# Six folds of the decode samples' projection, moved from VectorE adds to TensorE matmuls

## The chip, the cores and the metric

The kernel runs on one core of one Trainium2 chip. The metric is the device time of one execution in microseconds, and lower is better. A run's figure is the median of several executions.

## What is computed

The program is one inference step of a hybrid decoder layer. It has 1024 prompt rows and 8 decode samples (one token each). Every row of both kinds goes through the same combined input projection, and its columns then feed two head groups:

```python
shift, scale, gate = ada_modulation(c, w_ada, b_ada)
h = x * (1.0 + scale) + shift
z = h @ w_in                      # 1024 -> 2480 columns
cq, ckv, kr, g_mla, gq, gk, gv, glr, g_gla = jnp.split(z, offs, axis=-1)
q = rms_norm(cq, q_norm_g) @ w_uq          # latent attention, 8 heads
ckv, kr = rms_norm(ckv, kv_norm_g), apply_rope(kr, cos, sin)
mla = attention(q, ckv, kr) * silu(g_mla)
gla = rms_norm(gated_linear_attention(gq, gk, gv, log_sigmoid(glr @ w_gate_up + b_gate))) * silu(g_gla)
out = layer_norm(alpha * x + gate * (concat(mla, gla) @ w_out))
```

The change touches only the projection `h @ w_in` of the 8 samples. Everything is float32; the prompt's projection is made of three products of split operands (high times high, high times low, low times high).

## The kernel before

The order of the work on each engine is written out by hand, and semaphores (`wait_ge`, `then_inc`) tie the engines together. Each engine works through its own list strictly in order.

The input projection has six chunks of columns (`NCH`), of 416, 512, 512, 512, 272 and 256 columns (`WIDTH`). In chunk c, TensorE makes eight row tiles t of 128 prompt rows (`rows_projected(c, t)`, L1885, 24 matmuls each) into PSUM banks 0 to 5. ScalarE copies each tile out (`copy_tile`, L980). Between tiles the same engine also gets small pieces of other work:

- `samples_part(c + 1)` (L1858) projects the 8 samples on the raw weights of the next chunk. It makes eight matmuls with a 32-column stationary operand. The eight pieces of the inner dimension are spread over four groups of 32 partitions in PSUM bank 6, so that the samples' result is the sum of four partial results, on partitions 0 to 7, 32 to 39, 64 to 71 and 96 to 103.
- VectorE makes that sum: a copy (L1369) and three adds (L1372), each on 8 partitions, into `zs`. `sproj_part` counts the four steps, and `samples_part` of the chunk after waits for it, since it writes bank 6 again.
- `split_w` on ScalarE (L915) and `low_w` on VectorE (L1311) make the high and the low part of the next chunk's weights. VectorE's `low_w` stands behind the samples' sum in its list.
- `gate_samples` on ScalarE (L948) applies SiLU to `zs` in chunks 1 and 3.

In chunk 1 VectorE also normalizes the latent columns (L1379 to L1401), after `latent_norms` on ScalarE (L957 to L975).

Two other places of the kernel before already use the constant `fold`, a matrix of 128 by 32 with a one at each partition 32g + b, column b, so that `fold` transposed times a tile adds up its four groups of partitions: L2230 and L2478 make one and two such matmuls of 512 columns. A float32 matmul is recorded as two matmul records.

Of the kernel before, what the change touches and what calls it, by code (L numbers as in the profile page):

```python
# [104 lines left out]
def hybrid_step(nc, a, o):  # L105

    with ExitStack() as ctx:
# [67 lines left out]
        def carve(n, *dims, rows=P, at=None, region=None):  # L175

            region = C if region is None else region
            start = taken[0] if at is None else at
            taken[0] = start + n
            v = region[0:rows, start:start + n]  # L180
            if len(dims) > 1:
                names = "abcd"[:len(dims)]
                v = v.rearrange(f"p ({' '.join(names)}) -> p {' '.join(names)}",
                                **{k: d for k, d in zip(names, dims)})
            return v
# [10 lines left out]
        carve(512, region=F)  # L196
# [235 lines left out]
        sproj_gated = sem("sproj_gated")  # L432
# [471 lines left out]
        def _(act):  # L904
# [40 lines left out]
            def gate_samples(c):  # L945
                act.wait_ge(sproj_part, 4 * c + 4)
                cols = zs[:, CHUNKS[c][0]:CHUNKS[c][1]]
                nc.scalar.activation(cols, cols, ACT.Silu).then_inc(sproj_gated, 1)  # L948

            def latent_norms():  # L950
# [9 lines left out]
                act.wait_ge(sproj_part, 4)  # L960
# [22 lines left out]
            def copy_chunk(c):  # L983
                for t in range(T):
                    copy_tile(c, t)
                    if t == (3 if c == 0 else 2):
                        split_w(c + 1)
                    if c in (1, 3) and t == 0:
                        gate_samples(c)
# [292 lines left out]
            act.wait_ge(sproj_done, NCH + 1)  # L1282
# [16 lines left out]
        def _(dve):  # L1299
# [65 lines left out]
            for c in range(NCH):  # L1365
                n = WIDTH[c]
                cols = zs[:, CHUNKS[c][0]:CHUNKS[c][1]]
                dve.wait_ge(sproj_done, c + 1)
                nc.vector.tensor_copy(cols, banks[0:NB, 6, 0:n]).then_inc(sproj_part, 1)  # L1369
                for g in range(1, 4):  # L1370
                    dve.wait_ge(sproj_part, 4 * c + g)
                    nc.vector.tensor_tensor(cols, cols, banks[32 * g:32 * g + NB, 6, 0:n], ALU.add).then_inc(sproj_part, 1)  # L1372
# [370 lines left out]
            dve.wait_ge(sproj_done, NCH + 1)  # L1743
# [34 lines left out]
            dve.wait_ge(sproj_done, NCH + 2)  # L1778
# [24 lines left out]
        def _(pe):  # L1803
# [44 lines left out]
            def samples_part(c):  # L1848

                if c == 0:  # L1850
                    pe.wait_ge(hs_ready, 1)
                    brought(pe, 1, 4)
                else:
                    pe.wait_ge(w_in_in[c], 16)
                    pe.wait_ge(sproj_part, 4 * c)
                for kk in range(2):
                    for g in range(4):
                        last = nc.tensor.matmul(banks[32 * g:32 * g + 32, 6, 0:WIDTH[c]], hsT[:, 4 * kk + g, :],  # L1858
                                                w_raw[c][:, 4 * kk + g, :], start=(kk == 0), stop=(kk == 1))
                last.then_inc(sproj_done, 1)  # L1860

# [204 lines left out]
            for c in range(NCH):  # L2066
                for t in range(T):
# [8 lines left out]
                    if c == 0 and t == 3:  # L2076
                        samples_part(0)
                    if c + 1 < NCH and t == (5 if c == 0 else 2):
                        samples_part(c + 1)
                    if c == NCH - 1:  # L2080
                        if t == 0:
                            pe.wait_ge(proj_copied, T * (NCH - 1))
                            pe.wait_ge(sproj_part, 4 * NCH)
                            pe.wait_ge(sproj_gated, 2)
                            pe.wait_ge(const_in, N_CONST)
                            gate_rows(0)
# [436 lines left out]
```

## Time and profile before

| | before |
|---|---|
| median of 3 runs | 766.61 us (761.47 to 768.01) |
| profiled execution, its own time | 761.47 us |
| span of the profiled execution | 759.6 us |
| TensorE busy | 710.7 us, 94% of the span |
| VectorE busy | 354.3 us, 47% |
| ScalarE busy | 326.3 us, 43% |
| mean granted TensorE clock | 0.993 of full speed |

The span runs from the first to the last instruction; the execution's own time is 1.9 us longer. A matmul's recorded end is modelled, and matmuls overlap, so its price in a stream is read from the starts of its neighbours, not from its duration.

### The profile page before, as it was taken

What the parts mean: (1) busy time and instruction counts of PE and PEld (TensorE: products, weight loads), DVE (VectorE), ACT (ScalarE), POOL (GpSimd) and SP (SyncE); (2) the same over time, 40 slices, a digit from 0 to 9 for tenths busy, and PEclk for the clock granted to TensorE, in tenths of its full rate; (3) what the DMA queues carried; (4) which work ended last, traced back from release to release, by engine and by line L of the source; (5) the groups of instructions that cost most, each with busy time, mean ns of one, the idle gap of its engine ahead of it and who ended that gap; (6) DMA issues with size and microseconds to landing.
All of it is one profiled execution on the core that took longest, in us unless ns stands there. A gap on an engine that the chain in (4) does not pass through costs nothing.

```text
span 759.6 us, 16796 instructions
## 1 busy us (share of the span) xinstructions
PE 710.7 (94%) x7057; PEld 549.7 (72%) x7057; DVE 354.3 (47%) x774; ACT 326.3 (43%) x779; POOL 76.0 (10%) x113
## 2 busy tenths in 40 slices
PE   1699999999999999999989899999999999999995
PEld 1287878878789986777755577777668889668884
DVE  0372352030202025868666766675661111377967
ACT  2081471021203136776645555565666666602100
POOL 0000000000000010110121122002112443000000
PEclk9899999999999999999999999999999999999999
DMA  9992210302001011000010200021225996102332
GB/s 319 415 364 80 81 62 1 110 1 76 18 1 56 1 32 59 10 15 9 9 11 1 57 1 2 1 56 56 86 70 179 337 389 233 60 28 85 124 126 84
DMA packets 32086, 70.33 MB, mean 93 GB/s; under 512 B 6482, under 2 KB 17835, under 8 KB 29324
## 3 DMA queue, kind: packets, MB, share of 16 engines
q1 hardware_dynamic: 27386, 47.73, 18.8%
q0 software_dynamic: 4016, 20.97, 7.4%
q8 instruction: 57, 0.93, 0.5%
q10 hardware_dynamic: 610, 0.55, 0.3%
q14 instruction: 17, 0.14, 0.1%
HBM read 62.26 MB, written 6.07 MB: 90 GB/s over the span
## 4 chain that ended last, share of the span: by engine, by line
PE 85%; DMA 5%; DVE 4%; ACT 2%; SPq 2%; issue 1%; POOL 1%; DVEq 0%; ACTq 0%; POOLq 0%
PE banks L1885 28%; PE banks L2059 8%; PE banks L2164 4%; PE banks L2245 4%; DMA s_x<-in_x_prompt 3%; PE banks L2266 3%; PE banks L2028 3%; PE banks L2395 2%; PE banks L2397 2%; PE banks L2396 2%; PE banks L1965 2%; DMA s_temps<-in_cache_k_rope,s_idx 2%; PE banks L2378 2%; PE banks L2335 2%; PE banks L2354 1%; PE banks L2379 1%
## 5 line engine op out<-in xcount | busy, mean ns | idle before, releaser
L980 ACT ACTIVATE s_z<-banks 128x512 f32<-128x512 f32 (+3 forms) x48 | 24.5, 514 | 156.4 <-PE banks L1885 156.4
L1885 PE MATMUL banks<-s_w_parts,s_h_a 128*128 128x512 f32 (+3 forms) x352 | 81.0, 329 | 0.9 <-DVE s_h_a L1340 0.9
L1885 PE MATMUL banks<-s_w_parts,s_h_b 128*128 128x512 f32 (+3 forms) x352 | 80.1, 328 | 0.0
L1885 PE MATMUL banks<-s_z_r,s_h_a 128*128 128x512 f32 (+1 forms) x224 | 72.6, 389 | 0.0
L1885 PE MATMUL banks<-s_z_r,s_h_b 128*128 128x512 f32 (+1 forms) x224 | 71.8, 388 | 0.0
L1184 ACT ACTIVATE s_z<-banks 128x512 f32<-128x512 f32 (+1 forms) x88 | 41.3, 517 | 52.3 <-PE banks L2245 52.1
L1369 DVE COPY s_zs<-banks 8x512 f32<-8x512 f32 (+3 forms) x6 | 3.5, 576 | 123.7 <-PE banks L1858 123.7
L1885 PEld LDWEIGHTS banks<-s_w_parts,s_h_a 128*128 128x128 f32 x352 | 54.0, 189 | 8.1 <-issue 3.1
L1885 PEld LDWEIGHTS banks<-s_w_parts,s_h_b 128*128 128x128 f32 x352 | 54.0, 189 | 6.1 <-issue 1.5
L1885 PEld LDWEIGHTS banks<-s_z_r,s_h_a 128*128 128x128 f32 x224 | 42.0, 188 | 10.3 <-issue 1.7
L1175 ACT ACTIVATE s_z<-banks,s_temps 128x128 f32<-128x128 f32 (+7 forms) x64 | 47.1, 740 | 4.4 <-DVE s_temps L1636 3.7
L1885 PEld LDWEIGHTS banks<-s_z_r,s_h_b 128*128 128x128 f32 x224 | 42.0, 188 | 8.4
L2245 PEld LDWEIGHTS banks<-s_ident,s_z 128*128 128x128 f32 x288 | 33.5, 141 | 10.6 <-issue 5.4
L2245 PE MATMUL banks<-s_ident,s_z 128*128 128x128 f32 x288 | 39.7, 274 | 0.8 <-DVE s_z L1647 0.8
L2059 PE MATMUL banks<-s_kt,s_temps 96*128 96x512 f32 (+1 forms) x96 | 39.6, 534 | 0.0
L2164 PE MATMUL banks<-s_z 128*64 128x128 f32 x576 | 38.5, 278 | 0.8 <-ACT s_z L1184 0.8
L1194 ACT ACTIVATE s_z<-banks 128x512 f32<-128x512 f32 x64 | 33.1, 602 | 13.7 <-PE banks L2266 13.7
L2164 PEld LDWEIGHTS banks<-s_z 128*64 128x64 f32 x576 | 30.8, 136 | 6.2 <-issue 5.2
L1647 DVE TENSOR_SCALAR s_z<-s_z,s_temps 128x128 f32<-128x128 f32 (+7 forms) x64 | 33.3, 542 | 1.7
L1631 DVE TENSOR_REDUCE s_temps<-banks 128x1 f32<-128x640 f32 (+3 forms) x32 | 32.8, 1025 | 1.1
L2059 PE MATMUL banks<-s_kt,s_z 96*128 96x128 f32 (+2 forms) x96 | 32.3, 458 | 0.0
L1287 ACT ACTIVATE s_temps<-s_temps,s_eps_t 128x1 f32<-128x1 f32 (+1 forms) x9 | 2.7, 295 | 67.8 <-DVE s_temps L1766 67.8
(370 smaller groups left out, 1354.7 us busy)
## 6 DMA issues: line engine op xcount, KB each, us to landing
s_z<-in_w_ada SPq DMA_DIRECT2D x8, 1024.0 KB, 19.3
s_temps<-in_w_in SPq DMA_DIRECT2D x3, 2048.0 KB, 7.7
s_x<-in_x_prompt SPq DMA_DIRECT2D x8, 512.0 KB, 21.5
s_z<-in_w_ada SPq DMA_DIRECT2D x1, 4096.0 KB, 16.8
s_kt<-in_w_out SPq DMA_DIRECT2D x8, 512.0 KB
s_temps<-in_x_prompt SPq DMA_DIRECT2D x8, 512.0 KB
out_y_prompt<-s_temps SPq DMA_DIRECT2D x7, 512.0 KB
s_temps<-in_w_in SPq DMA_DIRECT2D x1, 1664.0 KB, 9.0
```

What stands on the lines that cost most here:

```text
L980: nc.scalar.activation(z[:, t, CHUNKS[c][0]:CHUNKS[c][1]], banks[:, proj_bank(c, t), 0:WIDTH[c]], ACT.Silu if c in (1, 3) else ACT.Copy).t ...
L1175: last = nc.scalar.activation(weights_of(s, u), score_of(s, u), ACT.Exp, bias=nmx[:, c:c + 1], accum_out=rsum[:, c:c + 1])
L1184: nc.scalar.activation(PTb[r % 3][:, 4 * g:4 * g + n, :], banks[:, 4 + (groups(r) + g) % 2, 0:P * n].rearrange("p (j q) -> p j q", j=n), A ...
L1194: nc.scalar.activation(latT(n, j), banks[:, j, :], ACT.Copy).then_inc(f_Tc, 1)
L1631: nc.vector.tensor_reduce(nmx[:, c:c + 1], score_of(s, 0), AX_X, ALU.max, negate=True).then_inc(mx_ready, 1)
L1647: last = nc.vector.tensor_scalar(weights_of(s, u), weights_of(s, u), rinv[:, c + u:c + u + 1], None, ALU.mult)
L1885: last = nc.tensor.matmul(banks[:, proj_bank(c, t), 0:WIDTH[c]], h_[half][:, k, n0:n0 + P], w_[c][:, k, :], start=(k == 0 and n == 0), sto ...
L2028: last = nc.tensor.matmul(banks[:, q_bank(i, q), 0:384], z[:, i, P * k:P * k + P], w_uq[:, k, 384 * q:384 * q + 384], start=(k == 0), stop ...
L2059: last = nc.tensor.matmul(score_of(s, u)[:, n0:n1], QTb[i % 2][:, h, :], KTh[:, h, n0:n1], start=True, stop=True)
L2164: last = nc.tensor.matmul(banks[64 * par:64 * par + 64, 6, 0:P], V(j, 2 * hp + par), block, start=(j == 0), stop=(j == i))
L2245: last = nc.tensor.transpose(banks[:, 4 + k0 % 2, P * (b % 4):P * (b % 4) + P], Pm[r % 3][:, P * b:P * b + P], ident[:])
L2266: last = nc.tensor.transpose(banks[:, j, P * r:P * r + P], cached(n, 4 * j + r), ident[:])
```

## The change

The sum of the four partial results moves from VectorE to TensorE. VectorE now makes one copy of all 128 partitions of bank 6 into SBUF (`zs_part`). TensorE multiplies it by `fold` (`samples_fold`) into bank 7, two row tiles after the samples' part (one tile after it for chunk 0). ScalarE copies the 8 rows from bank 7 into `zs` (`copy_samples`), with SiLU for chunks 1 and 3 on the way, in place of the separate SiLU. `sproj_done` now counts two steps for each chunk, and `sproj_copied` takes the place of `sproj_gated` and of the counts of `sproj_part`.

```diff
-        carve(512, region=F)
+        zs_part = carve(512, region=F)
...
-            def gate_samples(c):
-                act.wait_ge(sproj_part, 4 * c + 4)
-                cols = zs[:, CHUNKS[c][0]:CHUNKS[c][1]]
-                nc.scalar.activation(cols, cols, ACT.Silu).then_inc(sproj_gated, 1)
+            def copy_samples(c):
+                act.wait_ge(sproj_done, 2 * c + 2)
+                nc.scalar.activation(zs[:, CHUNKS[c][0]:CHUNKS[c][1]], banks[0:NB, 7, 0:WIDTH[c]],
+                                     ACT.Silu if c in (1, 3) else ACT.Copy).then_inc(sproj_copied, 1)
...
-                act.wait_ge(sproj_part, 4)
+                act.wait_ge(sproj_copied, 1)
...
-                    if c in (1, 3) and t == 0:
-                        gate_samples(c)
+                    if c == 0 and t == 5:
+                        copy_samples(0)
+                    if c == 1 and t == 0:
+                        copy_samples(1)
+                    if c >= 1 and t == (7 if c == 2 else 5):
+                        copy_samples(c + 1)
...
-                cols = zs[:, CHUNKS[c][0]:CHUNKS[c][1]]
-                dve.wait_ge(sproj_done, c + 1)
-                nc.vector.tensor_copy(cols, banks[0:NB, 6, 0:n]).then_inc(sproj_part, 1)
-                for g in range(1, 4):
-                    dve.wait_ge(sproj_part, 4 * c + g)
-                    nc.vector.tensor_tensor(cols, cols, banks[32 * g:32 * g + NB, 6, 0:n], ALU.add).then_inc(sproj_part, 1)
+                dve.wait_ge(sproj_done, 2 * c + 1)
+                nc.vector.tensor_copy(zs_part[:, 0:n], banks[:, 6, 0:n]).then_inc(sproj_part, 1)
...
-                    pe.wait_ge(sproj_part, 4 * c)
+                    pe.wait_ge(sproj_part, c)
...
+            def samples_fold(c):
+                pe.wait_ge(sproj_part, c + 1)
+                if c == 0:
+                    pe.wait_ge(mod_ready, 3)
+                else:
+                    pe.wait_ge(sproj_copied, c)
+                n = WIDTH[c]
+                nc.tensor.matmul(banks[0:32, 7, 0:n], fold[:], zs_part[:, 0:n], start=True, stop=True).then_inc(sproj_done, 1)
...
+                    if c == 0 and t == 4:
+                        samples_fold(0)
...
+                    if c + 1 < NCH and t == (7 if c == 0 else 4):
+                        samples_fold(c + 1)
...
-                            pe.wait_ge(sproj_part, 4 * NCH)
-                            pe.wait_ge(sproj_gated, 2)
+                            pe.wait_ge(sproj_copied, NCH)
```

The later waits on `sproj_done` are only renumbered.

On TensorE, in chunk 1, at the border from row tile 4 to row tile 5 (`s_z_r` and `s_w_parts` hold the weights' parts, `s_h_b` the second half of the rows), the list before is:

```order
L1885 MATMUL banks<-s_w_parts,s_h_b 128x512
L1885 MATMUL banks<-s_z_r,s_h_b 128x512
L1885 MATMUL banks<-s_z_r,s_h_b 128x512 [waits proj_copied]
L1885 MATMUL banks<-s_w_parts,s_h_b 128x512
L1885 MATMUL banks<-s_z_r,s_h_b 128x512 x2
```

and now it is:

```order
L1894 MATMUL banks<-s_w_parts,s_h_b 128x512
L1894 MATMUL banks<-s_z_r,s_h_b 128x512
L1869 MATMUL banks<-s_front,s_fold 32x512 [waits sproj_copied,sproj_part]
L1894 MATMUL banks<-s_z_r,s_h_b 128x512 [waits proj_copied]
L1894 MATMUL banks<-s_w_parts,s_h_b 128x512
L1894 MATMUL banks<-s_z_r,s_h_b 128x512 x2
```

One fold (L1869, reading `zs_part` in `s_front`) now stands between two tiles; nothing was taken from TensorE's list.

On VectorE, behind the normalization of chunk 1, the list before is:

```order
L1401 TENSOR_TENSOR s_zs<-s_zs,s_front 8x32 [waits kr_turned]
L1369 COPY s_zs<-banks 8x512 [waits sproj_done]
L1372 TENSOR_TENSOR s_zs<-s_zs,banks 8x512 [waits sproj_part] x3
L1311 TENSOR_TENSOR s_w_parts<-s_temps,s_z_r 128x2048 [waits w_hi_ready] x2
```

and now it is:

```order
L1401 TENSOR_TENSOR s_zs<-s_zs,s_front 8x32 [waits kr_turned]
L1372 COPY s_front<-banks 128x512 [waits sproj_done]
L1315 TENSOR_TENSOR s_w_parts<-s_temps,s_z_r 128x2048 [waits w_hi_ready] x2
```

The three adds are gone, and the copy goes to `s_front` on 128 partitions; it stands where the old copy stood, and the fold of chunk 2 waits for it.

## Rows read from the trace of the kernel before

**Rows 1.** Windows of the projection: us, busy us of each engine, clock, DMA
```profile
core 0: us, PE busy (x) PEld busy (x) DVE busy (x) ACT busy (x) POOL busy (x), PEclk, DMA share, GB/s
60.00:90.00 30.00, 30.00 (x184) 23.77 (x184) 10.84 (x12) 6.08 (x7) 0.00 (x0) 1.00 0.20 70
90.00:138.00 48.00, 48.00 (x218) 37.80 (x217) 14.92 (x32) 21.18 (x56) 0.00 (x0) 1.00 0.13 45
...
184.00:239.00 55.00, 55.00 (x295) 45.39 (x293) 4.13 (x6) 10.29 (x17) 0.00 (x0) 1.00 0.19 52
```

**Rows 2.** Waits from 60 to 257 us: us in total, times, longest
```profile
ACT s_z L980 <- PE banks L1885: 138.5, 34, 7.8
DVE s_zs L1369 <- PE banks L1858: 123.7, 5, 38.4
```

**Rows 3.** The chain that ended last, 60 to 275 us: shares and a piece
```profile
by line: PE banks L1885 92.8%; PE banks L1858 4.3%; PE banks L1844 1.7%; PE banks L1927 0.6%; PE banks L1942 0.2%; PE banks L1941 0.2%; PE banks L1922 0.2%; PE banks L1914 0.1%
...
109.29 44.57 PE banks L1885 x192
```

**Rows 4.** TensorE at chunk 1's start and a samples' part: start us, us, what
```profile
90.64 0.40 PE L1885 MATMUL banks<-s_z_r,s_h_a 128*128 128x512 f32 x1
...
106.81 0.39 PE L1885 MATMUL banks<-s_w_parts,s_h_a 128*128 128x512 f32 x1
107.04 0.40 PE L1885 MATMUL banks<-s_z_r,s_h_a 128*128 128x512 f32 x1
107.37 1.92 PE L1858 MATMUL banks<-s_temps,s_hsT 128*32 128x512 f32 x16
109.22 0.50 PE L1885 MATMUL banks<-s_z_r,s_h_a 128*128 128x512 f32 x1
109.56 0.39 PE L1885 MATMUL banks<-s_w_parts,s_h_a 128*128 128x512 f32 x1
```

**Rows 5.** Timeline of TensorE around the two folds of L2478
```profile
675.37 0.39 PE L2379 MATMUL banks<-s_z_r,s_w_parts 128*128 128x512 f32 x1
675.69 1.90 PE L2478 MATMUL banks<-s_z,s_fold 128*32 128x512 f32 x4
677.52 0.50 PE L2378 MATMUL banks<-s_z_r,s_w_parts 128*128 128x512 f32 x1
```

**Rows 6.** Timeline of TensorE around the single fold of L2230, and its durations
```profile
542.75 1.04 PE L2230 MATMUL banks<-s_z,s_fold 128*32 128x512 f32 x2
543.72 1.55 PE L2059 MATMUL banks<-s_kt,s_temps 96*128 96x512 f32 x3
...
L2230 PE MATMUL banks<-s_z,s_fold x2: 592/604/617, 542.7 to 543.2; 128*32 128x512 f32 x2
```

**Rows 7.** Timeline of TensorE in chunk 5, tiles 0 to 2
```profile
254.50 3.03 PE L1885 MATMUL banks<-s_w_parts,s_h_a 128*128 128x256 f32 x24
257.38 0.27 PE L1914 MATMUL banks<-s_ident,s_z 128*16 128x128 f32 x1
...
260.44 0.69 PE L1927 MATMUL banks<-s_w_gu,s_temps 17*128 17x256 f32 x2
...
264.04 0.27 PE L1914 MATMUL banks<-s_ident,s_z 128*16 128x128 f32 x1
```

**Rows 8.** VectorE: a group of the adds, and the timeline around the sums
```profile
L1372 DVE TENSOR_TENSOR s_zs<-s_zs,banks 8x512 f32<-8x512 f32 x9 | 6.1, 683 | 0.3
...
81.59 0.68 DVE L1369 COPY s_zs<-banks 8x512 f32<-8x512 f32 x1 [8.70 <-PE banks L1858]
...
84.35 4.47 DVE L1311 TENSOR_TENSOR s_w_parts<-s_temps,s_z_r 128x2048 fp32r<-128x2048 f32 x2
...
110.55 0.68 DVE L1369 COPY s_zs<-banks 8x512 f32<-8x512 f32 x1
```

**Rows 9.** ScalarE: timeline, and a copy of 8 rows out of PSUM
```profile
81.73 0.91 ACT L980 ACTIVATE s_z<-banks 128x416 f32<-128x416 f32 x2
...
L1278 ACT ACTIVATE s_zs<-banks x2: 569/570/572, 656.0 to 657.0; 8x512 f32<-8x512 f32 x2
```

More of the change, by code:

```diff
@@ L431, in hybrid_step @@
         sproj_done = sem("sproj_done")
-        sproj_gated = sem("sproj_gated")
+        sproj_copied = sem("sproj_copied")
         silu_done = sem("silu_done")
@@ L1281, in _ @@
             high_mixed(2)
-            act.wait_ge(sproj_done, NCH + 1)
+            act.wait_ge(sproj_done, 2 * NCH + 1)
             nc.scalar.activation(y_part, banks[:, 6:8, :].rearrange("p b n -> p (b n)"), ACT.Copy).then_inc(gate_bc, 1)
@@ L1742, in _ @@
             low_mixed(2)
-            dve.wait_ge(sproj_done, NCH + 1)
+            dve.wait_ge(sproj_done, 2 * NCH + 1)
             for k in range(KT):
@@ L1777, in _ @@
             r8, all_cols = slice(0, NB), slice(0, D)
-            dve.wait_ge(sproj_done, NCH + 2)
+            dve.wait_ge(sproj_done, 2 * NCH + 2)
             added(0, r8, all_cols, gateS, 6)
```

## The prediction

> **What bounds the kernel now.** I read the busy time by windows first, over the stretch from 60 to 239 us in which all six samples' sums are made or prepared. In each of the three windows shown TensorE's busy time equals the window (30 of 30, 48 of 48, 55 of 55 us), at full granted clock, 2.4 GHz [rows 1]. VectorE and ScalarE are busy for 4 to 15 us and 6 to 21 us there.
>
> Busy matmuls can still hide a wait, so the waits come second. From 60 to 257 us the list holds no TensorE matmul that waits for VectorE or ScalarE. It is the others that wait for TensorE: ScalarE 138.5 us for row tiles, and VectorE 123.7 us in total for the samples' parts, up to 38.4 us at a time [rows 2].  Third, the chain that ended last: from 60 to 275 us it lies on TensorE alone, 92.8% on the row tiles of L1885 and 4.3% on the samples' parts [rows 3]. A row tile of 512 columns takes 44.57 / 8 = 5.57 us in that chain.
>
> So the stage lasts as long as TensorE's list. Time taken from VectorE is worth nothing here unless TensorE would have waited for it, and time given to TensorE is paid in full.
>
> **What the change removes.** The 18 adds on VectorE go: nine of 512 columns take 6.1 us at 683 ns [rows 8], the other nine (416, 272 and 256 columns) about 3.8 us more, estimated by their columns. All of that lay in VectorE's slack, since VectorE then waited for the next samples' part. Worth of it on the path: 0. What could be late next is `low_w`, which stands behind the sum: for chunk 1 it ran from 84.35 for 4.47 us [rows 8], to 88.8, and chunk 1 starts at 90.64 [rows 4]. It was already in time by 1.8 us, and it now ends about 1 us earlier (3 x 0.68 = 2.0 us of adds less, 1.0 us of delay from the fold ahead of it). Two SiLU passes on ScalarE go too; they become part of the new copies. Worth 0.
>
> **What it adds on VectorE and ScalarE.** The copy grows from 8 to 128 partitions. Its bounds from the rows are 0.68 us for 512 columns on 8 partitions and about the same for an add of this length; partitions work side by side, so I take 0.68 us, hence no change. ScalarE gets six copies of 8 rows, less two SiLU passes; one of 512 columns out of PSUM took 570 ns [rows 9]. That is some 2 us net in an engine that waits 138.5 us for row tiles. Worth 0.
>
> **The new waits.** Each fold waits for VectorE's copy, and (from chunk 1 on) for ScalarE's copy of the chunk before. Behind it in TensorE's queue stand all row tiles, so a late partner would stop everything. The places, in the times of before:
> - Fold 1 stands after tile 7 of chunk 0, so just before 90.64 [rows 4] plus one us. VectorE's copy ends at about 82.3 [rows 8]. ScalarE's copy of chunk 0 stands behind the tile copies that began at 81.73 [rows 9] and ends near 83.2. Slack: 8 us.
> - Fold 2 is the tightest on VectorE, which holds it behind the latent normalization. The old copy started at 110.55 [rows 8], so the new one ends near 111.3, or near 112.5 with the delay of two folds. Its samples' part ended at 109.22 [rows 4] and two tiles of 5.57 us follow, so TensorE comes to the fold near 120.4, plus the same delay. Slack: 9 us.
> - For folds 3 to 5 VectorE is idle when the part ends, so the copy is done within 1 us of it, and two tiles follow, 11 us of 512 columns or 6 us of 272 columns (a 256-column tile lasts 257.38 - 254.50 = 2.88 us [rows 7]).
> - At the start of chunk 5 TensorE waits for all six sample copies. The last stands on ScalarE behind the copy of tile 5 of chunk 4 and ahead of two more tile copies for which TensorE already waits there. Nothing new.
>
> So all waits are met and cost 0. The transfers of the weights are issued after the same row tiles as before and slide with them.
>
> **What it adds on TensorE: six folds.** I price them by starts of neighbours. In the stream, a record of 512 columns starts every 0.23 us (106.81 to 107.04). Going into the samples' part that step is 0.33 us, and the second step after it is 0.34 us (109.22 to 109.56), so the two edges add 0.10 + 0.11 = 0.21 us [rows 4]. The two folds of L2478 hold the engine from 675.69 to 677.52, 1.83 us for four records [rows 5]; with the edges 2.04 us. The single fold of L2230 holds it from 542.75 to 543.72, 0.97 us for two records [rows 6]; with the edges 1.18 us. The difference of the two is two records: 0.86 us, 0.43 us each, and what is left over once for each insertion is 0.31 us.
>
> A fold of 512 columns is thus 0.86 + 0.31 = 1.17 us. By columns, 416 gives 0.70 + 0.31 = 1.01, 272 gives 0.46 + 0.31 = 0.77, and 256 gives 0.43 + 0.31 = 0.74. The last has a check: the small float32 matmul of 256 columns at L1927 stretched its tile from 2.88 us to 264.04 - 260.44 = 3.60 us, so 0.72 us [rows 7]. The sum:
>
> 3 x 1.17 + 1.01 + 0.77 + 0.74 = 6.0 us, all on the path.
>
> Bounds: without any cost at the edges it is 6.0 - 6 x 0.31 = 4.1 us. If the two records of a fold didn't overlap at all, each would take its recorded 0.60 us [rows 6] in place of 0.43; scaled by columns that adds 0.34 us for each 512 columns, over 2480 columns in all 1.6 us, so 7.7 us. I take 6.0, since the three places that it rests on agree within 0.03 us.
>
> The Trainium skill's "TensorEngine Tiling (Array Packing)", section Key Properties, says that changing the tiling mode drains the engine. The trace agrees: the 0.31 us are paid where 128*32 records stand between 128*128 ones. By the rule alone, folds placed right behind a samples' part, in the same mode, would save it and the sum would be near the lower bound; here each stands between two row tiles.
>
> **The sum.** The profiled execution took 761.47 us, so 767.5 us, a ratio of 1.0079. The median of the three runs shown is 766.61 us, and that execution was the fastest of the three. On the median the same 6.0 us give **772.6 us**, which I forecast. About 1% (7.7 us) is what a measurement of this kernel can tell from no change, so this is a loss that is just too small to be told with certainty.
>
> **Rivals.**
> 1. *The folds are hidden.* TensorE's weight loads are busy for 37.80 of 48 us, or 79% [rows 1], and in the samples' part 16 records of 512 columns take 1.85 us (107.37 to 109.22 [rows 4]), 0.12 us each, since four groups of 32 columns run side by side. If a fold's records cost only this, 12 of them cost 1.4 us and the time is 768.0 us, no change. Against it: all folds write the same group of 32 columns (partitions 0 to 31), they have no partner to run beside, and L2478 shows 0.43 us for such a record. The point from which it decides is whether the next row tile may start during a fold. The Trainium skill says in "Perfetto Trace Analysis", Identifying the Most-Contended Engine, that matmul busy time is a poor measure of how near TensorE is to its limit, and that weight-load busy time is a better one; by it there would be a fifth of room here, and this rival is what it would make of the change. The spacing of 0.23 us for 512 columns at full clock speaks against the room. Chance 0.06.
> 2. *The freed VectorE pays.* If the low weight parts had held TensorE at chunk borders, the adds would give up to 3 x 0.68 = 2.0 us back at each of five borders, 10.2 us against 6.0, so 762.4 us, faster. It decides if `low_w` ends after the chunk starts. It ends 1.8 us before at the border of chunk 1, the tightest, and no TensorE wait is listed. Chance 0.03.
> 3. *A fold stalls TensorE.* This ends clearly slower. The place is fold 2, where VectorE's copy is queued behind a normalization that itself waits for ScalarE. It decides once that copy ends later than 120 us, 9 us later than now; each us beyond is paid in full. With the copy 12 us later it would cost 3 us, in all 9 us and 775.6 us. Nothing in the change delays VectorE so much. Chance 0.03.
> 4. *The folds are dearer.* At the upper bound of 7.7 us the time is 774.3 us, at the border of 1%. This is the upper end of the forecast rather than another mechanism.
>
> **How the numbers follow.** The forecast, a pure cost on TensorE between 4.1 and 7.7 us, has 0.88. The runs shown differ by 6.5 us, so a median of a few can be off by 2 to 3 us either way; the centre of 6.0 lies 1.7 us below the 1% border, so about a quarter of the forecast's chance, 0.22, lies beyond it, and the rest, 0.66, within 1%. With rival 3 slower gets 0.25. Within 1% gets 0.66 + 0.06 = 0.72. Rival 2 with scatter makes 0.03 for faster. The range goes from the lower bound less 3 us of scatter (766.6 + 4.1 - 3 = 767.7), taken to 767 for rival 1, to the upper bound with 3.5 us of scatter (766.6 + 7.7 + 3.5 = 777.8): 767 to 778 us.
>
> **What would show it.** In the changed kernel's profile: six fold matmuls, two records each, with 0.97 us from the first one's start to the next row tile at 512 columns; no TensorE wait for VectorE or ScalarE from 60 to 257 us; the chunk starts later by 2.2 us at chunk 1 (folds 0 and 1), and chunk 5 by the whole 6.0 us; VectorE's busy time down by about 10 us with longer waits for the samples' parts; everything behind the projection unchanged in length and moved by 6 us. The prediction is wrong if a fold costs TensorE well under 1 us at 512 columns, if one of them waits, or if a later stage gives time back, which I can't see from here, since it starts only when TensorE has finished the projection.

## Result and profile after

| | before | after |
|---|---|---|
| median | 764.39 us (20 runs, 759.5 to 771.52) | 769.17 us (20 runs, 765.84 to 777.85) |
| ratio | | 1.0082, 95% interval 1.006 to 1.0103 |
| profiled execution, its own time | 761.47 us | 771.46 us |
| span | 759.6 us | 769.7 us |
| mean granted TensorE clock | 0.993 | 0.985 |

The change makes the kernel slower: by 0.8% by the ratio, whose interval reaches from 0.6 to 1.0%, and by 4.8 us or 0.6% by the two medians. The loss of about 6 us that was forecast is 0.8%, so it lies within that interval. It is within the 1% that a few runs can't tell from no change; with 20 runs of each it can be told. The two profiled executions differ by more, 10 us, and why is part of the study.

The windows of the projection after (columns as in [rows 1], bounds moved with the work):

```profile
60.00:90.00 30.00, 30.00 (x182) 23.19 (x175) 7.06 (x6) 6.34 (x8) 0.00 (x0) 1.00 0.20 70
91.00:144.00 53.00, 53.00 (x232) 40.22 (x232) 12.88 (x29) 21.60 (x57) 0.00 (x0) 1.00 0.17 59
184.00:244.00 60.00, 60.00 (x315) 48.66 (x314) 2.94 (x4) 11.23 (x18) 0.00 (x0) 1.00 0.16 48
```

The waits after, from 60 to 263 us:

```profile
ACT s_z L980 <- PE banks L1894: 145.8, 35, 7.8
DVE s_front L1372 <- PE banks L1858: 136.4, 5, 42.5
```

TensorE still fills each window at full clock (30 of 30, 53 of 53, 60 of 60 us), and the list still holds no matmul of it that waits for VectorE or ScalarE. It does hold six weight loads of row tiles (PEld, 4.2 us in all) that are put down to ScalarE's tile copies; they are the loads behind the six folds, and what they mean is told with e12. Against [rows 2] the other engines wait longer: ScalarE by 7.3 us, VectorE by 12.7 us, of which about 6 us are the longer stage. The time that the adds gave up has become waiting too.

The chain that ended last, after, from 60 to 281 us:

```profile
by line: PE banks L1894 90.7%; PE banks L1858 4.1%; PE banks L1869 2.2%; PE banks L1844 1.6%; PE banks L1936 0.6%; PE banks L1931 0.4%; PE banks L1951 0.2%; PE banks L1950 0.2%; PE banks L1923 0.1%
...
74.41 0.81 PE banks L1869 x2
...
91.09 0.98 PE banks L1869 x2
92.07 16.82 PE banks L1894 x72
...
122.03 0.97 PE banks L1869 x2
...
216.44 0.57 PE banks L1869 x2
```

In [rows 3] the row tiles and the samples' parts follow each other without a gap; now the folds of L1869 lie in the chain too, 2.2% of it.

TensorE's timeline after, around fold 1 and fold 2:

```profile
90.75 0.35 PE L1894 MATMUL banks<-s_w_parts,s_h_b 128*128 128x416 f32 x1
91.03 1.05 PE L1869 MATMUL banks<-s_front,s_fold 128*32 128x512 f32 x2
92.00 0.50 PE L1894 MATMUL banks<-s_z_r,s_h_a 128*128 128x512 f32 x1
92.34 0.39 PE L1894 MATMUL banks<-s_w_parts,s_h_a 128*128 128x512 f32 x1
...
121.63 0.40 PE L1894 MATMUL banks<-s_z_r,s_h_b 128*128 128x512 f32 x1
121.95 1.05 PE L1869 MATMUL banks<-s_front,s_fold 128*32 128x512 f32 x2
122.93 0.50 PE L1894 MATMUL banks<-s_z_r,s_h_b 128*128 128x512 f32 x1
123.27 0.40 PE L1894 MATMUL banks<-s_w_parts,s_h_b 128*128 128x512 f32 x1
```

The starts read as they did around L2230 and L2478 [rows 5, 6]. Fold 2 comes 0.32 us behind its neighbour (instead of 0.23), holds the engine for 0.98 us, and the step behind it is 0.34 us. Above the usual steps that is 0.09 + 0.98 + 0.11 = 1.18 us.

VectorE after, the group of the new copies (columns as in [rows 8]):

```profile
L1372 DVE COPY s_front<-banks 128x512 f32<-128x512 f32 (+3 forms) x6 | 3.5, 589 | 136.4 <-PE banks L1858 136.4
```

**The measure used below.** The whole time scatters by several us, so each experiment is read by a *stretch* of its chain first: from the start of the first gate-column matmul (L1844 in the kernel before) to the start of row tile 1 of chunk 5. It contains all six folds. Before it is 257.65 - 60.55 = 197.10 us, after it is 262.98 - 59.84 = **203.14 us**: 6.04 us more. Two further runs show how well it repeats: the kernel before once more gave 197.09 us, the changed one once more 203.13 us.

### The profile page after: what moved, and what is told of

Read it like the earlier page. It is cut to its first block, busy times and chain, and to the rows that moved or that the text cites. A ratio compares the mean times of both kernels' runs of the same rounds, so it can differ in the third digit from the quotient of the medians.

```text
span 769.7 us, 16811 instructions
## 1 busy us (share of the span) xinstructions
PE 723.2 (94%) x7069; PEld 553.8 (72%) x7069; DVE 343.9 (45%) x756; ACT 327.5 (43%) x783; POOL 75.5 (10%) x113
## 4 chain that ended last, share of the span: by engine, by line
PE 86%; DMA 4%; DVE 3%; ACT 2%; SPq 2%; issue 1%; POOL 0%; DVEq 0%; ACTq 0%; POOLq 0%
PE banks L1894 28%; PE banks L2068 8%; PE banks L2176 4%; PE banks L2257 4%; PE banks L2278 3%; DMA s_x<-in_x_prompt 3%; PE banks L2037 3%; PE banks L2407 2%; PE banks L2409 2%; PE banks L2408 2%; PE banks L1974 2%; PE banks L2347 2%; PE banks L2366 2%; PE banks L2390 2%; PE banks L2391 1%
## 5 line engine op out<-in xcount | busy, mean ns | idle before, releaser
L1372 DVE COPY s_front<-banks 128x512 f32<-128x512 f32 (+3 forms) x6 | 3.5, 589 | 136.4 <-PE banks L1858 136.4
L1894 PEld LDWEIGHTS banks<-s_z_r,s_h_b 128*128 128x128 f32 x224 | 42.0, 188 | 10.4 <-ACT s_z L980 1.7
```

Of the source, the lines that this page charges most:

```text
L1894: last = nc.tensor.matmul(banks[:, proj_bank(c, t), 0:WIDTH[c]], h_[half][:, k, n0:n0 + P], w_[c][:, k, :], start=(k == 0 and n == 0), sto ...
```

## Experiments

### The two halves of the change

**e1_folds_only**: the kernel before, with its adds, and six float32 folds of another tile into bank 7 at the places of the change. Their results are used by nobody.

```diff
+            def extra_fold(c):
+                if c == 0:
+                    pe.wait_ge(mod_ready, 3)
+                n = WIDTH[c]
+                nc.tensor.matmul(banks[0:32, 7, 0:n], fold[:], modB[:, 0:n], start=True, stop=True)
...
+                    if c == 0 and t == 4:
+                        extra_fold(0)
...
+                    if c + 1 < NCH and t == (7 if c == 0 else 4):
+                        extra_fold(c + 1)
```

> The kernel before with its VectorE adds kept, and six extra fold matmuls on a constant tile at the places of the changed kernel; their result is not used, and they wait for nothing but the gate's bias once. Measure: the stretch of TensorE from the first gate-column matmul (chunk 0) to row tile 1 of chunk 5, 197.1 us before and 203.1 us in the changed kernel. Theory A (the folds' TensorE time is the whole effect, 6.0 us; VectorE's and ScalarE's part is worth 0): 203.1 us, and 1.008 of the kernel before. Rival B (the folds cost more, say 8 us, and the freed VectorE or ScalarE gives 2 us back): 205 us, 1.0105. Rival C (the folds are free, and the loss comes from the new waits and copies): 197.1 to 198.5 us, 1.000 to 1.002.

Measured: stretch 203.14 us, the changed kernel's to 0.01 us. Median 774.04 us, ratio 1.012 (1.0071 to 1.0168).

**e2_no_adds**: the kernel before without its 18 adds. It leaves three of the four partial sums of the samples out; the waits on `sproj_part` are renumbered to fit.

```diff
                 nc.vector.tensor_copy(cols, banks[0:NB, 6, 0:n]).then_inc(sproj_part, 1)
-                for g in range(1, 4):
-                    dve.wait_ge(sproj_part, 4 * c + g)
-                    nc.vector.tensor_tensor(cols, cols, banks[32 * g:32 * g + NB, 6, 0:n], ALU.add).then_inc(sproj_part, 1)
```

> The kernel before without the 18 adds on VectorE: each samples' part is only copied from partitions 0 to 7, so three of the four partial sums are left out. Theory A: VectorE's time is off the path, the stretch stays 197.1 us, ratio 1.000. Rival B: the stretch is shorter by 1 to 2 us or a later stage gains, ratio 0.997 to 0.999. Either way VectorE's busy time falls by about 10 us.

Measured: stretch 197.09 us, median 764.69 us, ratio 0.999 (0.9968 to 1.0012). VectorE's busy time fell from 354.3 to 344.2 us and bought nothing. Its wait for the samples' parts (123.7 us in [rows 2]) took it up:

```profile
DVE s_zs L1369 <- PE banks L1855: 131.2, 5, 40.6
```

So the folds on TensorE are the whole cost, and the freed VectorE is worth nothing: rival 2 is out.

### What a fold's price consists of

**e3_folds_twice**: the changed kernel, each fold made twice in a row.

```diff
+                nc.tensor.matmul(banks[0:32, 7, 0:n], fold[:], zs_part[:, 0:n], start=True, stop=True)
                 nc.tensor.matmul(banks[0:32, 7, 0:n], fold[:], zs_part[:, 0:n], start=True, stop=True).then_inc(sproj_done, 1)
```

> The changed kernel with each fold made twice in a row (the second overwrites the first with the same values). Theory A (0.43 us for each record of 512 columns, and 0.31 us once for each place where a fold stands between row tiles): 12 more records but no new place, so 2480 columns x 2 x 0.84 ns = 4.2 us more than the changed kernel, stretch 207.3 us, 1.0135 of the kernel before. Rival D (the records cost little, the change of tile shape costs nearly all): 0.5 to 1.5 us more, 204 to 204.6 us. Rival E (each fold pays its own edge even when the next is also a fold): 6.0 us more, 209.1 us, 1.016.

Measured: stretch 207.27 us, 4.13 us above the change; ratio 1.0175 (1.0134 to 1.0216). Its timeline of TensorE at the start of chunk 1 (L1895 is the row tiles):

```profile
92.11 1.04 PE L1869 MATMUL banks<-s_front,s_fold 128*32 128x512 f32 x2
92.99 1.02 PE L1870 MATMUL banks<-s_front,s_fold 128*32 128x512 f32 x2
93.95 0.50 PE L1895 MATMUL banks<-s_z_r,s_h_a 128*128 128x512 f32 x1
```

An *edge* is what an insertion costs once, above its records, 0.31 us in the prediction. The second fold adds 0.88 us, and no edge. Twelve records more cost 4.13 us over 2480 columns, 0.43 us for a record of 512.

**e4_fold_beside_part**: folds 0 to 4 moved right ahead of the next samples' part, so that they share its edges; fold 5 stays. ScalarE's copies of the samples move with the folds (not shown).

```diff
-                    if c == 0 and t == 4:
-                        samples_fold(0)
                     if c + 1 < NCH and t == (5 if c == 0 else 2):
+                        samples_fold(c)
                         samples_part(c + 1)
-                    if c + 1 < NCH and t == (7 if c == 0 else 4):
-                        samples_fold(c + 1)
+                    if c == NCH - 2 and t == 4:
+                        samples_fold(NCH - 1)
```

> The changed kernel with folds 0 to 4 moved to stand right ahead of the next chunk's samples' part, so that 128*32 matmuls stand together; fold 5 stays alone. ScalarE's copies move with them. Theory A with the edge paid for changing the tile shape: five edges of 0.31 us saved, 1.5 us less than the changed kernel, stretch 201.6 us, 1.006 of the kernel before. Rival F (the 0.31 us belong to the float32 matmul itself or to its semaphore): nothing saved, 203.1 us, 1.008.

Measured: stretch 201.46 us, 1.68 us less than the change for five edges, 0.34 us each; ratio 1.0083 (1.0054 to 1.0111). Its timeline at the samples' part in chunk 1 (L1867 the fold, L1856 the part, L1892 the row tiles):

```profile
107.77 0.40 PE L1892 MATMUL banks<-s_z_r,s_h_a 128*128 128x512 f32 x1
108.09 0.62 PE L1867 MATMUL banks<-s_front,s_fold 128*32 128x512 f32 x1
108.11 0.63 PE L1856 MATMUL banks<-s_temps,s_hsT 128*32 128x512 f32 x3
108.55 0.59 PE L1867 MATMUL banks<-s_front,s_fold 128*32 128x512 f32 x1
108.56 2.29 PE L1856 MATMUL banks<-s_temps,s_hsT 128*32 128x512 f32 x13
110.79 0.50 PE L1892 MATMUL banks<-s_z_r,s_h_a 128*128 128x512 f32 x1
```

There is one step of 0.32 us in (107.77 to 108.09) and one of 0.33 us out (the next record of the row tile starts at 111.12) for both together.

**e7_gate_beside_part**: the kernel before, with the gate columns (L1844, float32, 128*32) moved down one tile, next to the first samples' part. No fold is in it: it asks whether an edge of the kernel before can be saved too.

```diff
-                    if c == 0 and t == 2:
-                        gate_columns()
                     if c == 0 and t == 3:
+                        gate_columns()
                         samples_part(0)
```

> The kernel before with the gate's columns moved from behind row tile 2 of chunk 0 to behind tile 3, right ahead of samples' part 0, so that two blocks of 128*32 matmuls stand together. Theory A (edges are paid where the tile shape changes): one edge less, 0.3 us less. Measured from the start of row tile 1 of chunk 0 to row tile 1 of chunk 5, 206.2 us before: 205.9 us. Rival (no such edge): 206.2 us. The whole execution can't tell either from no change.

Measured: since the gate columns move, the stretch is read from tile 1 of chunk 0, and it is 205.86 us against 206.19 before, 0.33 us less. Median 764.44 us, ratio 0.9991 (0.9965 to 1.0017). It is the only version that shortens the stretch of the kernel before by more than the 0.01 us to which it repeats; in the whole time so little can't be told.

**e6_fold_f32r**: the changed kernel with each float32 fold replaced by two fp32r products, of a high and a low part of `zs_part`, with an fp32r copy of `fold` as the stationary operand. VectorE makes the low part with one more operation.

```diff
-                nc.tensor.matmul(banks[0:32, 7, 0:n], fold[:], zs_part[:, 0:n], start=True, stop=True).then_inc(sproj_done, 1)
+                nc.tensor.matmul(banks[0:32, 7, 0:n], fold_r[:], zs_hi[:, 0:n], start=True, stop=False)
+                nc.tensor.matmul(banks[0:32, 7, 0:n], fold_r[:], zs_lo[:, 0:n], start=False, stop=True).then_inc(sproj_done, 1)
```

> The changed kernel with each float32 fold replaced by two matmuls of type fp32r, on the high and the low part of the copy; VectorE makes the low part with one more subtraction. Theory A (a record's price is its time in the array: 0.43 us for 512 float32 columns, 0.23 us for 512 fp32r columns as the row tiles show, and 0.31 us for the edges): 2480 columns x 2 x 0.45 ns = 2.2 us and 6 x 0.31 = 1.9 us, 4.1 us over the kernel before, stretch 201.2 us, 1.005 of the kernel before. Rival (each insertion has a fixed price whatever the type): 203.1 us, 1.008.

Measured: stretch 199.32 us, only 2.22 us above the kernel before, where 201.2 was expected; ratio 1.0058 (1.0028 to 1.0088). TensorE's timeline at the start of chunk 1 (L1874 and L1875 the products, L1900 the row tiles):

```profile
90.72 0.35 PE L1900 MATMUL banks<-s_w_parts,s_h_b 128*128 128x416 f32 x1
90.90 0.39 PE L1874 MATMUL banks<-s_front_parts,s_fold_r 128*32 128x512 f32 x1
91.13 0.39 PE L1875 MATMUL banks<-s_zs_lo,s_fold_r 128*32 128x512 f32 x1
91.36 0.40 PE L1900 MATMUL banks<-s_z_r,s_h_a 128*128 128x512 f32 x1
91.59 0.39 PE L1900 MATMUL banks<-s_w_parts,s_h_a 128*128 128x512 f32 x1
```

The steps run 0.18, 0.23, 0.23, 0.23 us. Each product costs what a record of a row tile costs, and there is no edge, though the records carry the same 128*32 as the folds. That was my miss: I had put the edge down to the form alone.

**e9_wide_float32**: the mirror case. The kernel before, with six float32 matmuls at the folds' places whose stationary operand has 128 columns (an identity). Their results are used by nobody.

```diff
+                nc.tensor.matmul(banks[:, 7, 0:n], ident[:], modB[:, 0:n], start=True, stop=True)
```

> The kernel before with six extra float32 matmuls at the folds' places and of the folds' column counts, but with a stationary operand of 128 columns (the identity), so that the tile shape 128*128 stays and only the type changes from fp32r to float32; the result is not used. The run with fp32r folds of shape 128*32 showed no edge at all, which speaks against the tile shape as its cause. Theory H (the 0.31 us at the edges are paid for a float32 matmul between fp32r ones): the stretch from the first gate-column matmul to row tile 1 of chunk 5 is 203.1 us, as with the folds. Theory A as first stated (paid for the change of shape): 197.1 + 4.2 = 201.3 us.

Measured: stretch 201.22 us, 4.12 us above the kernel before; ratio 1.0086 (1.0053 to 1.0119). The records cost what they cost in e3, and again there is no edge, so theory H is out. Neither float32 alone nor 32 columns alone brings the edge; among the added matmuls only the float32 ones of 32 columns have it.

**e12_padded_fold**: the same on the change's own folds: their stationary operand is padded with zeros to 128 columns.

```diff
+            nc.vector.tensor_copy(fold_w[:, 0:32], fold[:]).then_inc(mod_ready, 1)
+            nc.vector.memset(fold_w[:, 32:P], 0.0).then_inc(mod_ready, 1)
...
-                nc.tensor.matmul(banks[0:32, 7, 0:n], fold[:], zs_part[:, 0:n], start=True, stop=True).then_inc(sproj_done, 1)
+                nc.tensor.matmul(banks[:, 7, 0:n], fold_w[:], zs_part[:, 0:n], start=True, stop=True).then_inc(sproj_done, 1)
```

> The changed kernel with its folds' stationary operand padded from 32 to 128 columns (96 columns of zeros, made once on VectorE), so that the six folds keep their float32 records and places but are recorded as 128*128, like their neighbours. In the stretch of the chain from the first gate-column matmul to row tile 1 of chunk 5, the kernel before takes 197.1 us and the changed one 203.1. Theory A (0.43 us for a record of 512 columns, plus about 0.31 us once for each insertion of 32-column float32 records among 128-column ones): no insertion cost, so 197.1 + 4.1 = 201.2 us. Rival (the 0.31 us belongs to waiting on another engine's semaphore or to the place, not to the records' form): 203.1 us. In the whole time, about 768.5 against 764.4 for the kernel before, a ratio near 1.0055 by theory A and 1.008 by the rival, which the scatter may not tell apart; the stretch decides.

Measured: stretch 261.79 - 60.57 = 201.22 us, as theory A had it. Four times as many columns are computed and the fold is cheaper by 0.32 us. Since place, waits and data are those of the change, the edge belongs to the form of the records and not to a wait. Median 768.18 us, ratio 1.0098 (1.0065 to 1.013); that is more than the 1.0055 expected, and the part on the rest of the time comes back to it. Its timeline of TensorE at the start of chunk 1 (L1897 is the row tiles):

```profile
91.15 0.35 PE L1897 MATMUL banks<-s_w_parts,s_h_b 128*128 128x416 f32 x1
91.34 1.02 PE L1872 MATMUL banks<-s_front,s_fold_w 128*128 128x512 f32 x2
91.80 0.79 PE L1897 MATMUL banks<-s_z_r,s_h_a 128*128 128x512 f32 x1
92.43 0.39 PE L1897 MATMUL banks<-s_w_parts,s_h_a 128*128 128x512 f32 x1
```

From 91.34 to 92.43 there are 1.09 us for two records and one of a row tile, 0.86 + 0.23; the step in is the usual 0.19 us of a record of 416 columns, where the 32-column fold shows 0.28 us (90.75 to 91.03).

**What the weight loads show.** Each matmul record has a weight load ahead of it, listed under PEld. In the change, around fold 2:

```profile
121.41 0.19 PEld L1894 LDWEIGHTS banks<-s_z_r,s_h_b 128*128 128x128 f32 x1
121.95 0.14 PEld L1869 LDWEIGHTS banks<-s_front,s_fold 128*32 128x32 f32 x2 [0.36 <-issue]
122.93 0.19 PEld L1894 LDWEIGHTS banks<-s_z_r,s_h_b 128*128 128x128 f32 x1 [0.84 <-ACT s_z L980]
```

and in e12, around fold 1:

```profile
91.16 0.38 PEld L1872 LDWEIGHTS banks<-s_front,s_fold_w 128*128 128x128 f32 x2
91.77 0.19 PEld L1897 LDWEIGHTS banks<-s_z_r,s_h_a 128*128 128x128 f32 x1 [0.24 <-issue]
```

In a row tile a load starts a step ahead of its matmul (121.41 for 121.63). At the 32-column float32 fold it doesn't: the fold's load and matmul both start at 121.95, and the next row tile's both at 122.93, after the fold. With the padded fold the loads run ahead again (91.16 for 91.34, and 91.77 while the fold's second record is still under way), and so they do in e6 (90.72 and 90.91 for 90.90 and 91.13). So the edge comes with a load that isn't made during the matmul before it. The ScalarE named in the wait of 0.84 us is not its cause: the same gap stands behind the samples' part of the kernel before, with `issue` in its place (109.22).

The kernel before has another float32 record with this gap, L1927 of [rows 7], with 17 partitions and all 128 columns:

```profile
260.44 0.29 PEld L1927 LDWEIGHTS banks<-s_w_gu,s_temps 17*128 17x128 f32 x2
261.06 1.26 PEld L1885 LDWEIGHTS banks<-s_w_parts,s_h_a 128*128 128x128 f32 x10 [0.33 <-ACT s_z L980]
```

Both loads start with their matmuls (260.44 and 261.06), and the insertion costs the 0.72 us of the prediction, where e9's 128*128 insertion of 256 columns costs 0.43 us (249.23 to 249.67 in its chain). So among float32 records it isn't the 32 columns as such: 17 partitions bring an edge too.

### The cover of the waits

**e5_no_cover**: the changed kernel with each fold right behind its own samples' part, without the row tiles between them.

```diff
-                    if c == 0 and t == 4:
+                    if c == 0 and t == 3:
                         samples_fold(0)
...
                         samples_part(c + 1)
-                    if c + 1 < NCH and t == (7 if c == 0 else 4):
                         samples_fold(c + 1)
```

> The changed kernel with every fold made right behind its own samples' part, with no row tile between them. Theory A says that the two tiles between cover VectorE's copy: without them TensorE waits at each fold for the copy (0.58, three times 0.68, 0.43 and 0.41 us) and about 0.2 us of signalling, 4.7 us in all, and at fold 2 for VectorE's normalization too, about 1.3 us, while the folds lose one edge each (6 x 0.2 = 1.2 us less). Stretch from the first gate-column matmul to row tile 1 of chunk 5: 203.1 + 4.7 + 1.3 - 1.2 = 207.9 us, 1.014 of the kernel before. Rival (the waits are hidden by the matmuls queued in TensorE, or the copy is far quicker): 201 to 203 us.

Measured: stretch 209.29 us, 6.15 above the change and 1.4 above what was expected; ratio 1.0158 (1.0119 to 1.0198). Its waits from 60 to 263 us now hold what was absent in both kernels:

```profile
PE banks L1869 <- DVE s_front L1372: 5.3, 6, 1.9
```

The longest is at fold 2, the place that rival 3 named. TensorE's part of the timeline there:

```profile
110.34 1.92 PE L1858 MATMUL banks<-s_temps,s_hsT 128*32 128x512 f32 x16
114.14 1.05 PE L1869 MATMUL banks<-s_front,s_fold 128*32 128x512 f32 x2 [1.88 <-DVE s_front L1372]
```

and VectorE's, where the copy is queued behind the latent normalization:

```profile
113.31 0.18 DVE L1401 TENSOR_TENSOR s_zs<-s_zs,s_front 8x32 f32<-8x32 f32 x1
113.42 0.67 DVE L1372 COPY s_front<-banks 128x512 f32<-128x512 f32 x1
```

The windows around it say where the 1.4 us are (columns as in [rows 1]; the clock is the third figure from the end):

```profile
108.00:113.00 5.00, 4.27 (x27) 2.04 (x25) 4.93 (x18) 3.00 (x4) 0.00 (x0) 1.00 0.00 0
113.00:118.00 5.00, 3.85 (x10) 2.46 (x11) 4.93 (x6) 1.64 (x1) 0.00 (x0) 0.77 0.00 0
118.00:124.00 6.00, 6.00 (x25) 4.79 (x25) 0.49 (x1) 0.60 (x1) 0.00 (x0) 0.91 0.00 0
```

Behind the 1.88 us of idleness the granted clock fell from 2.4 to 1.2 GHz for a while, so that it is 0.77 and 0.91 of full speed on the average of these windows. The low stretch itself, cut out by the starts of TensorE's records, is 3.4 us long:

```profile
115.70:119.10 3.40, 3.40 (x10) 2.63 (x9) 2.79 (x2) 0.00 (x0) 0.00 (x0) 0.50 0.00 0
```

Half of it, 1.7 us, is lost (by the wider windows 5 x 0.23 + 6 x 0.09 = 1.7 us as well), and 209.29 - 1.7 = 207.6 us is near the 207.9 expected. With that fall the wait of 1.9 us cost about 3.6 us. One profile shows this; the five shorter waits (3.4 us in all) had no such fall behind them. The two row tiles of cover are what keeps all of this away in the change.

### The rest of the time

After has 769.7 - 262.98 = 506.7 us from the end of the stretch to the end of the span, before has 759.6 - 257.65 = 501.95. Nothing there was changed. These 4.8 us less 0.7 us of an earlier first gate column, plus 6.04, are the 10.1 us between the spans. The windows after, behind the projection:

```profile
389.00:394.00 5.00, 2.90 (x15) 1.94 (x15) 4.79 (x15) 2.45 (x11) 2.45 (x5) 1.00 0.28 29
394.00:399.00 5.00, 4.67 (x30) 3.80 (x31) 1.67 (x9) 2.15 (x7) 1.04 (x4) 0.63 0.12 9
399.00:404.00 5.00, 4.80 (x18) 3.28 (x18) 2.97 (x12) 1.30 (x5) 0.00 (x0) 0.68 0.00 0
```

and TensorE's wait in the first of them:

```profile
393.98 0.64 PE L2046 MATMUL banks<-s_ident,s_z 128*96 128x128 f32 x4 [1.52 <-POOL s_z L854]
```

TensorE idles in 389 to 394 us, and in the next two windows the granted clock is 0.63 and 0.68. That is 5 x 0.37 + 5 x 0.32 = 3.5 us of full-speed work, most of the 4.8 us. The kernel before has the same gap at the same instruction, 5 us earlier, with 1.52 us of wait and 2.80 of 5 us busy (386 to 391), and there the clock stayed at 1.00. So the fall can come behind the gap and needn't. Three experiments bear on whether the change does it.

**e11_before_again**: the kernel before, unchanged.

> The kernel before itself, submitted as if it were another: it shows how far a ratio strays with nothing changed. Expected 1.000, within 0.997 and 1.003, and a mean clock of 0.989. If it comes out at 1.003 or more, the ratios of 1.010 and 1.012 for kernels whose stretch grew by 6.0 us (1.008) are scatter of the method.

Measured: stretch 197.09 us, ratio 0.9999 (0.9972 to 1.0025), and 506.2 us behind the stretch, as much as the changed kernel's.

**e8_change_again**: the changed kernel, unchanged.

> The changed kernel once more, on the chip of the other runs of this group. Theory A: the stretch from the first gate-column matmul to row tile 1 of chunk 5 is 203.1 us again, whatever the whole execution does, and the ratio to the kernel before is 1.008. Rival G (the change also costs time behind the projection, 2 to 3 us, as the first group's ratios of 1.012 and 1.0175 could mean): 1.011 or more, and the stages behind the projection are longer than those of the kernel before at the same granted clock.

Measured: stretch 203.13 us, 513.3 us behind it; ratio 1.0103 (1.0062 to 1.0145). The part behind the stretch thus differs by 4.3 and 6.6 us between two profiles of one kernel, and nothing can be read from one pair of them.

**e10_fp32r_filler**: the kernel before with 26 fp32r matmuls of the row tiles' own form at the folds' places, some 6 us of TensorE work of the ordinary kind. Their results are used by nobody.

```diff
+                for _ in range((4, 5, 5, 5, 4, 3)[c]):
+                    nc.tensor.matmul(banks[:, 7, :], h_hi[0][:, 0, 0:P], h_hi[0][:, 1, :], start=True, stop=True)
```

> The kernel before with 26 extra fp32r matmuls of 128*128 by 512 columns in TensorE's list at the six places of the folds (4, 5, 5, 5, 4, 3); the result is not used. They delay everything behind them as the folds do, by 26 x 0.232 = 6.0 us, but without any float32 record. Theory A: stretch 203.1 us, ratio 1.008 as for the changed kernel. Rival G2 (beyond their 6.0 us the folds also lower the granted clock later on, which the mean clocks of 0.986 with folds and 0.989 without could mean): here the mean clock is 0.989 and the ratio 1.008, below the 1.010 to 1.012 of the other kernels with folds. If the mere shift in time does it, the mean clock is 0.986 here too.

Measured: stretch 203.06 us, ratio 1.0114 (1.0075 to 1.0153). 5.97 us alone would make 1.0078, which is within the interval. Most ratios of kernels with added TensorE work lie 0.002 to 0.004 above what their stretch explains: e1, e3, e4, e6, e8, e9 and e12 too, though not e5. For e12 the interval leaves out the 1.0054 of its stretch, and for e3 it barely leaves out the 1.0133. The 20 runs of the changed kernel itself show no such excess (1.0082 against 1.0079). Since e10 holds no float32 fold, what lies above isn't something that folds do. The clock shows part of it: over all runs the time falls by about 5.2 us for 0.01 of mean clock within one kernel, and the mean clock is 0.9885 over the runs of the kernel before and 0.984 to 0.988 over those of kernels with added work (0.985 in e10), so about 1 us. Whether longer TensorE lists bring the falls, or these few runs met more of them, stays open, and so does the rest of the excess.

## Why the prediction was right, point by point

**The bound.** "The stage lasts as long as TensorE's list": right. The windows after show it, e1 gives the whole cost by TensorE's additions alone, and e2 the value 0 of VectorE's time.

**What is removed.** Worth 0: right, by e2 (197.09 against 197.10 us). VectorE's busy time fell by 10.4 us, where about 10 was said.

**The copy and ScalarE.** The 128-partition copies of 512 columns took at most 692 ns, those of 8 partitions at most 679 ns, so the 0.68 us held. TensorE never waited for ScalarE's copies.

**The waits.** All 0: right. Fold 2's slack was put at 9 us. In e5, which takes the cover of 11 us away, the fold waited 1.9 us, so the slack is indeed about 9 us.

**The price of a fold.** The stretch gives 6.04 us for the six, against 6.0. Fold by fold, the chain after less the chain before gives 1.00, 1.16 and 1.18 us for folds 0 to 2 and 0.74 us for fold 5, against 1.01, 1.17, 1.17 and 0.74. The split holds too: records 4.13 us (e3) and 4.12 us (e9, e12), against 4.1, and edges of 0.32 to 0.34 us (e12, e4, e7), against 0.31. The bound of 7.7 us for records that don't overlap can be dropped: e3 shows them overlap.

**What the edge is.** Only in part right. Behind the sum I had written that it is paid where 128*32 records stand between 128*128 ones. That holds for the float32 records of 128*32 here, and e12 shows the cure of making the form equal; but e6 has fp32r records of 128*32 between 128*128 ones without it, and the float32 record of 17*128 at L1927 has it without 32 columns. So the edge goes with float32 records of another form than their neighbours, and with weight loads that don't run ahead; why the fp32r ones are exempt stays open. No term of the sum hung on this. There was luck in one place: the check of 0.72 us was read from L1927, whose form isn't the fold's, and it fits because its records have an edge too.

The Trainium skill's rule in "TensorEngine Tiling (Array Packing)", Key Properties, that changing the tiling mode drains the engine, agrees with e4, e7, e9 and e12, and with the weight loads that start only with their own matmul. By its use in the prediction, folds right behind a samples' part should save the edge: they do in e4, which puts them ahead of it. For e6 the rule would need its fp32r products to run in the row tiles' mode, which no row shows; its loads do run ahead.

**Rival 1, hidden folds.** Wrong by 4.6 us: 1.4 us against 6.04. What the weight loads leave free, 21% of 48 us before [rows 1] and 23 to 24% after (they are busy for 23.19 of 30 and 40.22 of 53 us), is not room for matmuls; e10 fills the list with 26 ordinary ones and each of them is paid at 0.23 us.

So the rule that the rival rested on, weight-load busy time as the measure of TensorE's limit in the Trainium skill's "Perfetto Trace Analysis", Identifying the Most-Contended Engine, does not hold for this stage; the other measure that the same section names, the arithmetic done as a share of the peak, was not tried.

**Behind the projection.** "Unchanged in length" was too simple. The work is unchanged, but its length differs by 4 to 7 us between profiles of the same kernel, with the clock. The sum on the profiled execution gave 767.5 us and that execution took 771.46; on the medians, 764.39 to 769.17, the 6.0 us fit the measured 4.8 within the scatter of several us. The forecast of 772.6 us lay 3.4 us above the median after, of which 2.2 us are the base: three runs had given 766.61, twenty gave 764.39. The other 1.2 us are the 6.0 less the 4.8.

## What to carry to other kernels

Before work is moved from a waiting engine to another, look whether the receiving engine is the bound: here 10 us of VectorE time were worth nothing and 6 us of TensorE time were paid in full. Price an insertion by the starts of its neighbours, in records plus edges, and read it again in a stretch of the chain that ends before the clock starts to wander, which repeated to 0.01 us where medians scattered by several. If a float32 matmul with few columns in its stationary operand must stand among wide ones, pad that operand to their width, or put it next to one of its own kind; look at the weight loads to see whether they run ahead again.

## What was not expected of the hardware

- The fold of two fp32r products costs 2.22 us in six places where the float32 one costs 6.04: 0.23 against 0.43 us for a record of 512 columns, and no edge at all.
- A fold that computes 128 columns is cheaper than one that computes 32 (4.12 against 6.04 us in all).
- A copy out of PSUM costs VectorE the same on 128 partitions as on 8 (692 and 679 ns for 512 columns at most).
- Behind one wait of 1.88 us TensorE ran at 1.2 GHz for 3.4 us, so that the wait cost nearly twice its length. Behind a wait of 1.52 us the clock fell in the profile after (0.63 and 0.68 over 10 us) and not in the one before.
- Weight loads stop running ahead around a float32 matmul of another form than its neighbours; that, and not its records, is where the 0.3 us of an edge lie.
